# Moving attention head ends one step later and three VectorE modulation units to TensorE in a two-model fp32 kernel

## What is computed

```python
for i in range(2):                       # the kernel calls them layers i = 1 and i = 2
    mod = silu(c) @ ada_w[i] + ada_b[i]  # 1024 -> 6144: shift1, scale1, gate1, shift2, scale2, gate2
    h = rmsnorm(x, norm1_g[i]) * (1 + scale1) + shift1
    y = diff_attention(h, ...)           # i = 1: 8 heads, two softmaxes each, w = p0 - lam * p1,
                                         #        then rmsnorm(o) * subln_g per head, then @ w_o
        or axial_gqa(h, ...)             # i = 2: 8 query heads, 2 key/value heads, one softmax each, @ w_o
    x = x + gate1 * y
    h = rmsnorm(x, norm2_g[i]) * (1 + scale2) + shift2
    x = x + gate2 * swiglu(h, f_w_in[i], f_w_out[i])
```

## Time and profile before

| | |
|---|---|
| median of 3 runs | 1323.96 us (1323.85 to 1324.6) |
| the profiled execution | 1323.34 us, of which the span of the trace is 1321.6 us |
| PE busy | 1133.0 us (86%) |
| DVE busy | 674.9 us (51%) |
| ACT busy | 545.0 us (41%) |
| HBM traffic | 394.97 MB read, mean 301 GB/s over the span |
| layer i = 1, projections and attention | about 668 to 805 us of the span |
| layer i = 2, attention | about 1060 to 1104 us of the span |

### The profile page before, as it was taken

How to read it: one execution, slowest core, us unless ns; L and a number is a source line. 1 busy time by engine, 2 the same in 40 slices (tenths; PEclk the granted TensorE clock), 3 DMA queues, 4 the chain that set the end, 5 groups by cost and what they waited for, 6 DMA issues and landing times.

```text
span 1321.6 us, 19883 instructions
## 1 busy us (share of the span) xinstructions
PE 1133.0 (86%) x8439; PEld 848.3 (64%) x8439; DVE 674.9 (51%) x1415; ACT 545.0 (41%) x1185; POOL 0.2 (0%) x4
## 2 busy tenths in 40 slices
PE   6999999867666675756799889999999979999997
PEld 5777667634333442524467667788887768888886
DVE  4575665111111011101077766898876865776665
ACT  4554553111111111101165664666644754666653
POOL 0000000000000000000000000000000000000000
PEclk9999999998887977778899989999999989999999
DMA  9996947999999999999997416676757513655500
GB/s 391 421 426 247 392 160 294 428 426 427 427 426 428 422 428 427 427 427 427 426 397 283 184 64 261 274 293 274 296 216 294 232 57 139 243 191 191 191 32 32
DMA packets 29702, 397.36 MB, mean 301 GB/s; under 512 B 3496, under 2 KB 4904, under 8 KB 5416
## 3 DMA queue, kind: packets, MB, share of 16 engines
q1 hardware_dynamic: 29176, 395.72, 73.1%
q10 hardware_dynamic: 432, 0.30, 0.1%
HBM read 394.97 MB, written 1.05 MB: 300 GB/s over the span
## 4 chain that ended last, share of the span: by engine, by line
PE 56%; DMA 22%; DVE 14%; ACT 7%; issue 1%; ACTq 0%; DVEq 0%; SPq 0%
PE ps L1163 15%; DMA ring<-in_w13b 12%; PE ps L1164 8%; DMA mem<-in_w13b 6%; PE ps L1155 5%; PE ps L1156 4%; PE ps L1157 4%; ACT mem L1852 4%; DVE memr L2353 4%; DMA ring<-in_w 4%; PE ps L1680 3%; ACT memr L1852 3%; PE ps L1640 2%; DVE mem L2353 2%; PE ps L1735 2%; DVE mem L2359 2%
## 5 line engine op out<-in xcount | busy, mean ns | idle before, releaser
L2353 DVE TENSOR_TENSOR memr<-ring,memr 128x512 fp32r<-128x512 f32 x432 | 292.8, 689 | 168.0 <-ACT memr L1852 164.1
L1163 PE MATMUL ps<-memr 128*128 128x512 f32 x952 | 339.6, 400 | 3.9 <-DVE memr L2353 1.9
L1852 ACT ACTIVATE memr<-ring 128x512 fp32r<-128x512 f32 x432 | 264.4, 628 | 180.2 <-PE ps L1164 86.5
L1852 ACT ACTIVATE mem<-ps 128x512 f32<-128x512 f32 (+5 forms) x307 | 128.5, 439 | 392.7 <-PE ps L1680 232.3
L1164 PE MATMUL ps<-memr 128*128 128x256 f32 x952 | 267.3, 281 | 0.0
L1163 PEld LDWEIGHTS ps<-memr 128*128 128x128 f32 x952 | 178.8, 188 | 50.0 <-DVE memr L2359 5.9
L1155 PE MATMUL ps<-memr 128*128 128x256 f32 (+2 forms) x504 | 179.9, 357 | 6.8 <-DVE memr L2353 4.1
L1164 PEld LDWEIGHTS ps<-memr 128*128 128x128 f32 x952 | 179.8, 189 | 1.6
L2353 DVE TENSOR_TENSOR mem<-mem,ps 128x512 f32<-128x512 f32 (+1 forms) x76 | 43.5, 572 | 243.8 <-ACT mem L1852 243.8
L1156 PE MATMUL ps<-memr 128*128 128x256 f32 (+2 forms) x504 | 165.9, 329 | 0.0
L1157 PE MATMUL ps<-memr 128*128 128x256 f32 (+2 forms) x504 | 165.6, 329 | 0.0
(11 more groups left out here) (184 smaller groups left out, 1149.6 us busy)
## 6 DMA issues: line engine op xcount, KB each, us to landing
ring<-in_wpk SPq DMA_DIRECT2D x89, 2048.0 KB, 9.8
ring<-in_w13a SPq DMA_DIRECT2D x17, 2048.0 KB, 44.0
mem<-in_w13b SPq DMA_DIRECT2D x16, 2048.0 KB, 45.3
ring<-in_w SPq DMA_DIRECT2D x16, 2048.0 KB, 45.4
ring<-in_w13b SPq DMA_DIRECT2D x16, 2048.0 KB, 43.9
mem<-in_w13a SPq DMA_DIRECT2D x15, 2048.0 KB, 44.9
mem<-in_w SPq DMA_DIRECT2D x15, 2048.0 KB, 45.4
mem<-in_wpk SPq DMA_DIRECT2D x1, 2048.0 KB, 10.3
```

The source lines that it names most:

```text
L1163: te.matmul(ps[:, 0:512], a[0], b[1], start=start, stop=False)
L1852: return self.e.activation(out, src, f, **k)
L2353: return self.e.tensor_tensor(out, a, b, op)
```

## The change

The table `ADA` gets the three units (1,7), (1,8) and (1,9): (1,7) joins the group of (1,4) to (1,6), (1,8) and (1,9) form a new group of their own. `TURNED_1` and its generator go. The units move in the stream to where PE uses them, and PE multiplies them at three new places: (1,7) after (1,6), (1,8) after the first v projection, (1,9) between step 12 and the output projection. In `attention` the head's end moves from step 2h+5 to step 2h+6 and stands ahead of the next head's `a_values`; for i = 2 the loop without slabs runs one step longer, 13 for 12.

```diff
 ADA = (((0, 0), (0, 2)), ((0, 1), (0, 3)), ((0, 4), (0, 5), (0, 6), (0, 7), (0, 8), (0, 9)),
        ((0, 10), (0, 11), (1, 0), (1, 1), (1, 2), (1, 3)),
-       ((1, 4), (1, 5), (1, 6)), ((1, 11), (2, 0), (2, 1)),
+       ((1, 4), (1, 5), (1, 6), (1, 7)), ((1, 8), (1, 9)), ((1, 11), (2, 0), (2, 1)),
        ((2, 4), (2, 5)), ((2, 10), (2, 11)))
 TURNED_AT = (0, 2, 4, 5, 7, 9, 11)
-TURNED_1 = ((1, 7), (1, 8), (1, 9))
-TURNED_2 = ((1, 10), (2, 2), (2, 3), (2, 6), (2, 7), (2, 8), (2, 9))
-TURNED = TURNED_1 + TURNED_2
+TURNED = ((1, 10), (2, 2), (2, 3), (2, 6), (2, 7), (2, 8), (2, 9))
@@ unit_list
-    mixed((U_AQKV, 8), ada(1, 4), ada(1, 7), (U_AQKV + 2, 8), ada(1, 5), (U_AQKV + 4, 8), ada(1, 6),
-          (U_AQKV + 1, 8), ada(1, 8), (U_AQKV + 3, 8), (U_AQKV + 5, 8), ada(1, 9),
-          (U_AWO, 8), (U_AWO + 1, 8), ada(1, 11), ada(2, 0), ada(2, 1))
+    mixed((U_AQKV, 8), ada(1, 4), (U_AQKV + 2, 8), ada(1, 5), (U_AQKV + 4, 8), ada(1, 6), ada(1, 7),
+          (U_AQKV + 1, 8), ada(1, 8), (U_AQKV + 3, 8), (U_AQKV + 5, 8),
+          (U_AWO, 8), ada(1, 9), (U_AWO + 1, 8), ada(1, 11), ada(2, 0), ada(2, 1))
@@ attention
             if 2 <= step < 18:
                 self.a_turn(i, step - 2)
+            if step >= 6 and step % 2 == 0:
+                self.a_end(i, step // 2 - 3)
             if step >= 4 and step % 2 == 0 and step < 20:
                 self.a_values(i, step // 2 - 2)
-            if step >= 5 and step % 2:
-                self.a_end(i, (step - 5) // 2)
             yield
@@ layer2
         self.a_free = [(s.pe_moe, ("scatter", 7))]
-        self.slow = self.turned_units(TURNED_1, 5)
         self.side.append(self.second_norm())
         qk_unit("q10", 0, 0.125, m.qT1, 0, self.a_free)
         self.ada_unit(1, 5)
         qk_unit("k10", 1, 1.0, m.kT1, 0, self.a_free)
         self.ada_unit(1, 6)
+        self.ada_unit(1, 7)
         v_unit(0)
+        self.ada_unit(1, 8)
         self.side.append(self.paced(at, [1] * 8))
@@ layer2, after the last v projection
         self.drain()
         next(at)
+        self.ada_unit(1, 9)
         self.side.append(self.paced(at, [0] * 9))
@@ layer3
-        for step in range(12):
+        for step in range(13):
             if step == 8:
```

More of the change, by code:

```diff
@@ L425, in unit_list @@
             if i == 0 and n in TURNED_AT:
-                mixed(ada(*TURNED_2[TURNED_AT.index(n)]))
+                mixed(ada(*TURNED[TURNED_AT.index(n)]))
         if i == 0:
@@ L1084, in stages @@
         if i == 1:
-            p.slow = p.turned_units(TURNED_2, 4)
+            p.slow = p.turned_units(TURNED, 4)
         for n in range(11):
```

## The result

| | before | after |
|---|---|---|
| median, 7 runs each | 1323.85 us (1320.72 to 1324.60) | 1328.47 us (1325.59 to 1329.94) |
| the profiled execution | 1323.34, span 1321.6 | 1327.07, span 1325.3 |
| ratio of the times | | 1.0039, 95% interval 1.0029 to 1.0048 |

The changed kernel is slower by some 5 us, beyond the 2.65 us (0.2%) that I had called the bound of "no change". The number 1324.9 was 3.6 us low; 1328.47 lies at the upper end of the range.

A forecast was written before the change was run, and what follows sets the result against it. PE was taken to bound the first and last attention stretches, the DVE and ACT loop the middle. Layer 1 -1.3 and layer 2 +2.2 gave +0.9 us: 1324.2 for the profiled execution, 1324.9 for the median, range 1320.3 to 1328.5.

The forecast's parts named there:

- What bounds the kernel: Layer 1's attention: the loop of round trips between DVE and ACT sets the pace, 6.85 us per cycle.
- part 1: Layer 1: twelve DVE chunks go; five lie in DVE's side of the loop, -5.7 us, perhaps only -3.4.
- part 3: Layer 1, head ends one step later: 0 to +0.8 us up to the first add, taken as +0.75 for lower clock.
- Part 2: Layer 1: three units come to PE; (1,7) and (1,8) cost +3.7 us in a full queue, with no cover.
- Part 4: Layer 1's output projection: -1.75 us, but one 3.6 us wait brings lower clock, charged 1.7; taken as -0.05.
- Part 5: Layer 2, head ends one step later: +1.15 to head 4's scores, +0.15 cycle, +0.95 head 3; together +2.2 us.
- B: Rival: DVE's relief carries through and PE becomes the limit from 718 to 805 us; about 1319.5, milder 1320.8; chance 0.20.
- D: Rival: the chunks were hidden, PE's own queue sets the pace; up to 1332 us, half hidden 1327.5; chance 0.09.
- C: Rival: few long PE waits bring more lower-clock stretches, 1.7 us each; three more 1330 us, two 1328.3; chance 0.17.

The follow-up runs named there:

- e5: Changed kernel with layer 1's 128-feature sum of a head written to the upper half of the bank holding its values: 1327.29 us, 1.0033 of before.
- e6: Changed kernel with layer 1's late head end queued behind the next head's values instead of ahead of them: 1327.54 us, 1.0039 of before.
- e11: Kernel before with only the three units moved to PE: (1,7) behind q11, (1,8) behind k11, (1,9) just ahead of step 12: 1317.21 us, 0.9955.
- e10: Changed kernel with the last q's rope piece queued ahead of the attention step in layer 2: 1328.10 us, 1.0035 of before.
- e7: Kernel before with layer 2's head ends one step later, except head 3, which stays at step 11: 1326.38 us, 1.0028.
- e3: Kernel before with only the three modulation units on PE, head ends as before in both layers: 1322.82 us, 0.9999.
- e13: Changed kernel with 13 unread matmuls in PE's long wait in layer 1's output projection: 1327.14 us, 1.0031 of before.
- e4: Kernel before with the units on PE and late head ends in layer 1 only, layer 2 unchanged: 1326.59 us, 1.0024.
- e1: Kernel before with head ends one step later in layer 2 only: 1326.66 us, 1.0029.
- e12: Kernel before with the units on PE where the change puts them, and the 128-feature sum in the values' bank: 1321.75 us, 0.9992.
- e14: Changed kernel with the ends of layer 1's heads 4 to 7 back at odd steps, behind the values: 1328.49 us, 1.0043 of before.

## Why the prediction was wrong, step by step

**What bounds the kernel: right.** DVE and ACT's loop sets layer 1's attention; e5 and e6 exchanged 6.0 us of PE wait for others at 0.7 us of gain or none, and e11 put 3.7 us of PE work beside the loop for 1.3. PE's own work is not wholly off the path, though: a portion of lower clock at 766 us lengthened the cycle from step 8 to step 10 by 1.5 us in e10 (9.38 for 7.89).

**The base of part 1 and part 3: the first step that failed.** The forecast took its starting points from one execution in which the clock was low from 776 us on the earlier trace rows, and used 4.91 us from the maxima of step 12 to the first add. In e7, the same code at full clock, it is 3.25 us (maxima at 778.50, add at 781.75), and the whole stretch is 86.82 against 84.95. So 1.9 us of the relief lay in a disturbance of that execution, which the two other traces of the code do not have. That the execution as a whole was 0.6 us under the median hid this. I had even named the lower clock in that place as a cost of the new order and not seen that it was already in the base.

**The sizes in parts 1 and 3.** Counted from the first scores and against the clean base (e7), the maxima of step 12 come at 55.96 us in e3 for 60.69: the five chunks gave 4.73 us, not 5.7, between my two bounds (3.4 and 5.7). The late ends bring them to 55.60 in the changed kernel: -0.36, forecast -0.8. From there to the first add it takes 5.93 us for 3.25: +2.68, forecast 6.45 for 4.91, or +1.55. Together -2.41 up to the first add (61.53 for 63.94), forecast -4.95; against the disturbed base (65.82) it would be -4.29.

**Part 2: right.** +3.7 forecast, +3.46 measured. (1,9) is hidden with the late ends, as the 5.93 us show (5.7 forecast for the case that it is), and is not with early ones (5.30 in e3 for 3.25).

**Part 4: mechanism right, size off, the second step that failed.** One long wait, then a lower clock: 3.17 us of wait for 3.6 forecast, in five traces of six. But behind it I counted 8.1 us of work, and it is 9.3 at full clock. So the stretch from the first add is 20.36 (e13) for 19.25, and 21.96 with the fall for 20.95: +0.96 in place of -0.05. The price of the fall, 1.6 us (10.94 less 9.33), was forecast as 1.7.

**Part 5: right.** +2.2 forecast, +2.6 measured (57.41 to 60.02, two portions in each). The terms, counted from the first scores (1061.62 before, 1062.73 after): maxima of head 4 +1.26 (forecast 1.15), the next cycle 3.13 for 2.94 (+0.19, forecast 0.15), and to the end of step 12's work or head 3's last piece +2.54 in all, which leaves +1.1 for head 3 (forecast 0.95). In these two traces the transposes of q come only 0.54 us later, not 1.4, and the rest of the first term is the lower clock in the scores of head 4 (2.05 us for 1.13). But before had lost both its portions ahead of these transposes and after only one. e13, with the code of after in layer 2 and both portions ahead as before had them, bears the forecast's way out: the transposes come 15.21 us after the first scores (at 1059.57) for 13.91, +1.30, and the scores of head 4 17.08 for 15.98, +1.10, at full clock:

```profile
1074.78 1.09 PE L1460 MATMUL ps<-cst,mem 128*128 128x128 f32 x8 [1.96 <-DVE mem L2355]
1076.65 1.10 PE L1541 MATMUL ps<-mem 128*128 128x256 f32 x4 [0.78 <-ACT mem L1854]
```

Of the term of head 3, e7 gave back some 0.55 us at the same clock lost.

**What I had not seen:** the bank waits, 6.0 us of PE idle, cost at most 0.7.

**The sum again.** Layer 1: +3.46 - 2.41 + 0.96 = +2.0 us; layer 2: +2.6; together +4.6, and the medians differ by 4.62. That the two agree so closely is luck: single executions of one kernel differ by more than 2 us, and the two profiled ones differ by 3.73. Forecast were -1.3 and +2.2. The 3.3 us between -1.3 and +2.0 are the base (4.91 for 3.25: 1.7), part 4 (1.0), the chunks (1.0) and the -0.8 of the late ends (0.4), less 0.5 for the lower clock charged at step 12 and 0.2 in part 2. What stays open: by traces without clock lost the late ends cost layer 1 only 0.5 us (81.90 in e13 for 81.42 in e3) and the fall 1.6 more, and by the times of e4 and e3 they cost 0.25%, 3.3 us, with an interval that reaches down to about 1.6.

**The rivals.** B did not come: PE still waits over 10 us. D named the right sign, not the mechanism: the chunks were worth their cost in place (e3 stands at 0.9999). C is the nearest in time (1328.3 with two stretches), but not in cause: the one stretch in the output projection was in my sum already, and sixteen traces do not show that further ones became more frequent in layer 1: ahead of the output projection the clock lost is 1.5 us on average in the seven traces with early ends and 1.9 in the nine with late ones. In layer 2 there may be something in it: one or two portions in the seven with early ends, two or three in the nine with late ones, where one more costs 1.2 us (60.0 to 61.2). The Trainium skill's rule beside B (Perfetto Trace Analysis, "Identifying the Most-Contended Engine") says which engine to relieve first; e3 and e11 follow it alike, and one gains nothing and the other 6.0 us. The occupancy rows told the engine, the list of waits told the place.

## What to carry to other kernels

Before a forecast rests on a stretch of one trace, read its granted clock in 2-us windows: a portion of lower clock in the base looks like a gain of the change and is none. The same holds for two traces that are compared: count the portions in the stretch first (e7 and e1). Work moved to an engine is cheap where the waits of that engine lie (1.3 us for 3.7 beside the attention loop), and costs its full length a few us earlier; choose the place from the list of waits, as e11 does. Gathering many short waits into one long one can cost more than it looks, since a lower clock may follow; in e13 thirteen unread matmuls in the wait kept it up, by one trace.

## What the runs showed of the chip

The same instructions get the lower clock in one execution and not in the next. Three traces of one code from 668 to 805 us lost 5.12, 1.70 and 0.00 us of clock, and after and e10, the same code too, 1.70 and 5.12. What a portion costs depends on where it falls: 1.6 us in the output projection behind the long wait, 1.6 and 1.5 at 748 and 766 us in e10 (the first add comes 64.64 us after the first scores with these two before it, 61.53 in after with none), and 0.0 us at 774 us in e1 (against e7) and at 770 us in e5. The Trainium skill (TensorE: Matmul & The Clock Gate, "Part 1: The HAM clock gate") says of a kernel's start that the number of matmuls at the lower level varies from run to run; these traces show the like in the middle of a kernel. Runs of one kernel on one chip spread over 2.1 (e12) to 6.8 us (e14) here, which is one to four portions; that this is what spreads them is not shown. The mean clock of the whole execution goes with the time only weakly (correlation -0.3 over 82 executions of the kernel before).
